# A linear attention in levels of quarters in place of halves, a table cast in pieces, and a sum taken two steps sooner

## The reference

```python
def gla_scan(q, k, v, log_a, s0):
    ...
    def step(S, inp):
        qc, kc, vc, ac = inp
        bcum = jnp.cumsum(ac, axis=1)
        diff = bcum[:, :, None] - bcum[:, None, :]
        decay = jnp.exp(jnp.where(causal[None, :, :, None, None], diff, -jnp.inf))
        att = jnp.einsum('bijhd,bjhd->bhij', qc[:, :, None] * decay, kc)
        o = (jnp.einsum('bhij,bjhe->bihe', att, vc)
             + jnp.einsum('bihd,bhde->bihe', qc * jnp.exp(bcum), S))
        blast = bcum[:, -1]
        S = (jnp.exp(blast)[..., None] * S
             + jnp.einsum('bjhd,bjhe->bhde', kc * jnp.exp(blast[:, None] - bcum), vc))
        return S, o
```

## Time and profile before

| | us |
|---|---|
| median of 3 runs | 1818.34 (1818.22 to 1819.02) |
| the profiled execution | 1818.22, of which 1816.4 are the span |
| PE busy | 1785.9 |
| DVE, ACT, POOL busy | 748.9, 509.3, 513.1 |
| a tile of the linear attention | 40.82, seven times from 907.22 to 1192.96; the first 40.62 |

### The profile page before, as it was taken

The page is one execution under the profiler, slowest core; times in us unless marked ns, Lnnn a source line. Parts: engine busy times, 40 slices in busy tenths (PEclk is TensorE's granted clock), DMA queues, the critical chain, the costliest instruction groups (busy, mean ns, idle before and its releaser), DMA issues.

```text
span 1816.4 us, 30442 instructions
## 1 busy us (share of the span) xinstructions
PE 1785.9 (98%) x11013; PEld 1663.2 (92%) x11013; DVE 748.9 (41%) x1517; ACT 509.3 (28%) x1205; POOL 513.1 (28%) x438
## 2 busy tenths in 40 slices
PE   6999999999999999999999999999999999999999
PEld 5999999989999999999999999999999888878887
DVE  7655540454434411111455554543221453453433
ACT  6311110134333410000344344430011343333332
POOL 4255430322232243342444444443324000000000
PEclk8999999999999999999999999999999999999999
DMA  7323211343444331221333432244443675664653
GB/s 258 134 79 86 80 51 38 97 110 101 111 112 118 92 110 54 80 71 53 110 85 93 116 98 84 84 126 148 143 123 113 209 253 163 206 221 163 197 168 133
DMA packets 245804, 221.10 MB, mean 122 GB/s; under 512 B 25857, under 2 KB 210337, under 8 KB 244274
## 3 DMA queue, kind: packets, MB, share of 16 engines
q1 hardware_dynamic: 171794, 177.07, 31.3%
q10 hardware_dynamic: 73944, 43.15, 8.7%
HBM read 170.03 MB, written 52.24 MB: 122 GB/s over the span
## 4 chain that ended last, share of the span: by engine, by line
PE 95%; DVE 2%; DMA 1%; ACT 1%; issue 0%; SPq 0%; POOL 0%; ACTq 0%; DVEq 0%
PE p L1717 20%; PE p L1719 19%; PE p L1718 19%; PE p L1808 7%; PE p L1810 7%; PE p L1812 7%; PE p L838 3%; PE p L581 1%; PE p L1752 1%; PE p L1751 1%; PE p L1753 1%; PE p L609 1%; PE p L593 1%; PE p L849 1%; PE p L856 1%; PE p L850 1%
## 5 line engine op out<-in xcount | busy, mean ns | idle before, releaser
L1717 PE MATMUL p<-x_hi,w_lo 128*128 128x384 f32 x2016 | 699.5, 347 | 0.0
L1719 PE MATMUL p<-x_hi,w_hi 128*128 128x384 f32 x2016 | 676.1, 335 | 0.0
L1718 PE MATMUL p<-x_lo,w_hi 128*128 128x384 f32 x2016 | 675.2, 335 | 0.0
L1717 PEld LDWEIGHTS p<-x_hi,w_lo 128*128 128x128 f32 x2016 | 379.8, 188 | 15.4 <-issue 13.3
L1718 PEld LDWEIGHTS p<-x_lo,w_hi 128*128 128x128 f32 x2016 | 380.0, 188 | 0.2
L1719 PEld LDWEIGHTS p<-x_hi,w_hi 128*128 128x128 f32 x2016 | 379.1, 188 | 0.0
L537 POOL TENSOR_TENSOR w_hi<-raw,small 128x512 fp32r<-128x512 f32 x164 | 174.2, 1062 | 724.5 <-PE p L1719 724.2
L541 POOL TENSOR_TENSOR w_lo<-raw,w_hi 128x512 fp32r<-128x512 f32 x164 | 215.1, 1312 | 12.9
L1997 DVE TENSOR_TENSOR w_lo<-raw,w_hi 128x512 fp32r<-128x512 f32 x192 | 132.2, 691 | 205.0 <-ACT w_hi L1665 205.0
L1665 ACT ACTIVATE w_hi<-raw 128x512 fp32r<-128x512 f32 x192 | 120.6, 631 | 240.5 <-PE p L1812 213.2
L1808 PE MATMUL p<-w_hi,x_lo 128*128 128x512 f32 x576 | 162.1, 390 | 1.1 <-DVE w_lo L1997 1.1
(11 more groups left out here) (174 smaller groups left out, 1753.7 us busy)
## 6 DMA issues: line engine op xcount, KB each, us to landing
raw<-in_w_out SPq DMA_DIRECT2D x192, 256.0 KB, 3.3
raw<-in_w_in SPq DMA_DIRECT2D x164, 256.0 KB, 4.5
h_t<-xn SPq DMA_DIRECT2D x126, 192.0 KB, 1.9
work<-h_t SPq DMA_DIRECT2D x24, 384.0 KB, 6.0
out<-work SPq DMA_DIRECT2D x36, 256.0 KB, 4.5
work<-h_t ACTq DMA_DIRECT2D x16, 512.0 KB, 5.3
work<-h_t ACTq DMA_DIRECT2D x32, 256.0 KB, 3.7
work<-in_x_prompt SPq DMA_DIRECT2D x32, 256.0 KB, 4.9
```

Of the source, the lines that this page charges most:

```text
L1717: pe.matmul(out, w_lo[:, k, :], x_hi[:, k, tok], start=(k == 0), stop=False)
L1718: pe.matmul(out, w_hi[:, k, :], x_lo[:, k, tok], start=False, stop=False)
L1719: mm = pe.matmul(out, w_hi[:, k, :], x_hi[:, k, tok], start=False, stop=(k == KT - 1))
```

## The change

Levels are blocks of 4s tokens in quarters, for s = 32, 8 and 2, in place of halves of 64 to 1. At each level the queries of the second, third and fourth quarter meet the keys of the quarters before them: 6 of 16 quarter pairs, 192 columns a head (`PAIRS`). What is left is the diagonal and the pair of tokens 2m and 2m + 1; the odd queries, scaled by their own gate (`l_odd`), are put behind the queries, and the diagonal's product takes 192 columns a head (`SAME`). So a tile has 4 such products of 192 columns in place of 1 of 128 and 7 of 64, decode 3 in place of 5. POOL makes four subtractions a level, ACT two exps, DVE four multiplications and six masked copies. Keys are turned at step 18, values at 22, levels at 29, 33 and 41. In decode keys are at 16, two levels at 28 and 33, values at 38. The diagonal now waits for `l_odd`, whose exp ACT takes after DVE's gates and ahead of the load of the gates' inputs, the scaling, the store and the load of the values. The first level's buffers (`far` and the place of the tile's stored output) wait for that store (`sl_st`). DVE clears `far` once.

The table (now 2560 columns) is cast in five pieces of 512. In the item `J_ATT` alone, the last sum of squares of the item before is taken at k = 4 in place of 6, and the first scores at step 5 in place of 4.

```diff
-LEVELS = (64, 32, 16, 8, 4, 2, 1)
-DEC_LEVELS = (8, 4, 2, 1)
+LEVELS = (32, 8, 2)
+DEC_LEVELS = LEVELS[1:]
+SAME = 3 * P // 2
+PAIRS = 6 * P // 4
+QUAD_AT = (0, 3 * P // 4, 5 * P // 4)
...
+M_PIECE = 512
+N_PIECES = (M_ALL + M_PIECE - 1) // M_PIECE
...
+        l_qo = four(work[:, 0:N_GLA * SAME])
+        l_q, l_odd = l_qo[:, :, 0:P], l_qo[:, :, P:SAME]
...
+        same_bank = (ub[0], ub[4])
...
             def values():
                 pe.wait_ge(sl_v, 16 * t + 16)
                 pe.wait_ge(sl_on, 4 * t + 1)
+                if dec:
+                    pe.wait_ge(sl_cp, len(LEVELS) * t + 1)
...
             def diagonal():
                 pe.wait_ge(sl_q, 16 * t + 16)
                 pe.wait_ge(sl_k, 16 * t + 16)
-                pe.wait_ge(sl_la, t + 1)
+                pe.wait_ge(sl_la, 2 * t + 2)
+                pe.wait_ge(sl_og, 4 * t + 1)
                 for h in range(N_GLA):
-                    hs = slice(h * P, h * P + P)
-                    mm = pe.matmul(ub[0][:, hs], l_k[:, hs], l_q[:, hs], start=True, stop=True)
+                    mm = pe.matmul(same_bank[h // 2][:, (h % 2) * SAME:(h % 2) * SAME + SAME], l_k[:, h * P:h * P + P],
+                                   l_qo[:, h, :], start=True, stop=True)
                 mm.then_inc(sl_dg, 1)
...
             def level(i):
                 s = levels[i]
                 pe.wait_ge(sl_zz, NZ * t + (i + 3))
-                if i == 1:
+                if s == LEVELS[1]:
+                    pe.wait_ge(sl_on, 4 * t + 1)
+                    if not dec:
+                        pe.wait_ge(sl_vtok, 2 * t + 2)
+                else:
                     pe.wait_ge(sl_ktok, t + 1)
-                if i >= 2:
-                    pe.wait_ge(sl_cp, len(LEVELS) * t + (i - 1))
+                    pe.wait_ge(sl_dcp, t + 1)
+                    if s == LEVELS[2] and not dec:
+                        pe.wait_ge(sl_cp, len(LEVELS) * t + 1)
+                at = quad_bank(s)
                 for h in range(N_GLA):
-                    z = l_z[(i + 1) % 2][:, h * P:h * P + P]
-                    mm = pe.matmul(ub[4 - i % 2][:, h * 64:h * 64 + 64], z, halves(z, s)[:, :, 1, :],
-                                   start=True, stop=True)
+                    mm = pe.matmul(ub[at + h // 2][:, (h % 2) * PAIRS:(h % 2) * PAIRS + PAIRS],
+                                   l_k4[s][:, h * P:h * P + P], l_q4[s][:, h, :], start=True, stop=True)
                 mm.then_inc(sl_p, 1)
...
-            stages = {6: logits, 14: diagonal, 22: keys, 30: values, 47: outputs}
+            stages = {6: logits, 14: diagonal, 18: keys, 22: values, 47: outputs}
             if not first:
                 stages[9] = linear_stages(pe, t - 1)[-1]
-            for i, step in enumerate((23, 25, 28, 32, 35, 38, 42)):
+            for i, step in enumerate((29, 33, 41)):
                 stages[step] = lambda i=i: level(i)
...
+                act.wait_ge(sl_la, 2 * t + 1)
+                act.activation(l_odd, odd(four(l_e[1])), ACT.Exp, scale=1.0 / TAU).then_inc(sl_a, 1)
...
+                act.wait_ge(sl_d, (NZ - 1) * t + (i + 2))
+                e = blocks(l_k4[s], s)[:, :, 0:3 * s]
+                act.activation(e, e, ACT.Exp, scale=-1.0 / TAU)
+                e = l_q4[s].rearrange("p h n -> p (h n)")
+                self.exp(t, i + 2, e, e, 1.0)
...
                     self.load_v(t)
                     self.decays(t)
+                    self.keys(t)
                     self.level(t, 0, LEVELS[0])
-                    self.keys(t)
-                    for i in range(1, 4):
-                        self.level(t, i, LEVELS[i])
+                    self.values(t)
 
                 def part_1():
-                    self.values(t)
-                    for i in range(4, 7):
+                    for i in range(1, len(LEVELS)):
                         self.level(t, i, LEVELS[i])
 
                 def part_2():
...
+                dve.memset(far, 0.0)
...
-                dve.copy_predicated(l_att, tables_sb[:, M_DIAG:M_DIAG + 512], ub[0][:, :]).then_inc(sl_dcp, 1)
+                for h in range(2):
+                    ins = dve.copy_predicated(two_heads(l_att, h), two(tables_sb[:, M_DIAG:M_DIAG + 2 * P]),
+                                              two(same_bank[h][:, 0:2 * SAME])[:, :, 0:P])
+                    ins.then_inc(sl_half, 1)
+                for h in range(2):
+                    dve.wait_ge(sl_half, HALVES * t + (h + 1))
+                    dve.nop(nofuse=True)
+                    ins = dve.copy_predicated(odd(two_heads(l_att, h)), two(tables_sb[:, 0:M_QUAD]),
+                                              two(same_bank[h][:, 0:2 * SAME])[:, :, P:SAME])
+                ins.then_inc(sl_dcp, 1)
...
-                self.copy_diagonal(t)
+                dve.wait_ge(sl_a, 4 * t + 4)
+                dve.wait_ge(sl_q, 16 * t + 16)
+                dve.tensor_tensor(l_odd, odd(l_q), l_odd, ALU.mult).then_inc(sl_la, 1)
...
+                self.copy_diagonal(t)
...
+                z, k = (blocks(x, s)[:, :, 0:3 * s] for x in (l_k4[s], l_k))
+                dve.tensor_tensor(z, k, z, ALU.mult)
+                for b in range(3):
+                    z = paired(l_q4[s], s, b)
+                    ins = dve.tensor_tensor(z, later(l_q, s, b), z, ALU.mult)
+                ins.then_inc(sl_zz, 1)
...
+                for at, b in enumerate((0, 2) if one_seq else (0, 1, 2)):
+                    n = s if one_seq else (3 - b) * s
+                    for h in range(2):
+                        if at:
+                            dve.wait_ge(sl_half, done + (2 * at + h - 1))
+                            dve.nop(nofuse=True)
+                        ins = dve.copy_predicated(
+                            later(two_heads(l_att, h), s, b)[:, :, :, 0:n], paired(mask, s, b)[:, :, :, 0:n],
+                            paired(two(ub[quad_bank(s) + h][:, 0:2 * PAIRS]), s, b)[:, :, :, 0:n])
+                        if b < 2:
+                            ins.then_inc(sl_half, 1)
+                ins.then_inc(sl_cp, 1)
...
                 def part_0():
                     self.gates(t)
                     self.level(t, 0, LEVELS[0])
-                    for i in range(1, 4):
+
+                def part_1():
+                    for i in range(1, len(LEVELS)):
                         self.level(t, i, LEVELS[i])
                         self.take(t, i - 1, LEVELS[i - 1])
-
-                def part_1():
-                    for i in range(4, 7):
-                        self.level(t, i, LEVELS[i])
-                        self.take(t, i - 1, LEVELS[i - 1])
+                    self.take(t, 2, LEVELS[2])
 
                 def part_2():
-                    self.take(t, 6, LEVELS[6])
                     self.state(t)
                     self.variance(t)
...
-            for i, (n, at) in enumerate([(n, n - 1)] + [(2 * s, s - 1) for s in levels]):
-                if i:
-                    pool.wait_ge(sl_zz, NZ * t + i)
-                b = l_b.rearrange("p (m n) -> p m n", n=n)
-                pool.tensor_tensor(l_e[(i + 1) % 2].rearrange("p (m n) -> p m n", n=n), b,
-                                   b[:, :, at:at + 1].to_broadcast([P, 4 * P // n, n]), ALU.subtract)\
-                    .then_inc(sl_d, 1)
+            pool.wait_ge(sl_a, 4 * t + 4)
+
+            b = l_b.rearrange("p (m n) -> p m n", n=n)
+            pool.tensor_tensor(l_e[1].rearrange("p (m n) -> p m n", n=n), b,
+                               b[:, :, n - 1:n].to_broadcast([P, 4 * P // n, n]), ALU.subtract).then_inc(sl_d, 1)
+            for s in levels:
+                if s == LEVELS[1]:
+                    pool.wait_ge(sl_zz, NZ * t + 2)
+                    pool.wait_ge(sl_kt, t + 1)
+                else:
+                    pool.wait_ge(sl_st, 16 * t + 16)
+                    if s == LEVELS[2] and n == P:
+                        pool.wait_ge(sl_p, len(LEVELS) * t + 1)
+                e, b = (x.rearrange("p (m q n) -> p m q n", q=4, n=s) for x in (l_k4[s], l_b))
+                pool.tensor_tensor(e[:, :, 0:3, :], b[:, :, 0:3, :],
+                                   b[:, :, 0:3, s - 1:s].to_broadcast([P, P // s, 3, s]), ALU.subtract)
+                for c in range(3):
+                    x = later(four(l_b), s, c)
+                    ref = l_b.rearrange("p (h m n) -> p h m n", h=N_GLA, n=4 * s)[:, :, :, (c + 1) * s - 1:(c + 1) * s]
+                    ins = pool.tensor_tensor(paired(l_q4[s], s, c), x,
+                                             ref.to_broadcast([P, N_GLA, P // (4 * s), (3 - c) * s]), ALU.subtract)
+                ins.then_inc(sl_d, 1)
...
-                stages = {3: logits, 6: linear_stages(self.pe, T - 1)[-1], 12: diagonal, 18: keys, 32: values}
-                for i, step in enumerate((20, 22, 25, 28)):
+                stages = {3: logits, 6: linear_stages(self.pe, T - 1)[-1], 12: diagonal, 16: keys, 38: values}
+                for i, step in enumerate((28, 33)):
```

(76 more changed lines are left out.)

60 lines of the change are left out of this document (27 added, 33 removed).

## The result

The changed kernel takes 1829.88 us (median of 4 runs, 1826.74 to 1830.15), against 1818.28 of the kernel before: 1.0063 times the time, 95% interval 1.0048 to 1.0077. Slower by 0.6% or 11.6 us, where 7 us less were forecast. The profiled execution took 1829.84, its span is 1828.1.

What follows compares the result with a forecast made beforehand. PE, busy 98% of the span, was taken to bound the kernel. Terms 1.8 - 0.1 - 0.7 + 5.1 + 1.1 gave 7.2 us less than the profiled 1818.22, so 1811.0, range 1801 to 1820.

Steps and rivals of the forecast that it cites:

- the sum 1.8 - 0.1 - 0.7 + 5.1 + 1.1: Gains in us: seven later tiles, first tile, decode, the cast in pieces, the sooner sum in `J_ATT`; together 7.2.
- Products: PE's stages in a linear-attention tile: 192 columns cost 1.31 each, so 1.96 us less a tile.
- The values' wait: Values' stage moved from step 30 to 22: load lands at 17.1 in the tile, PE waits 1.7 us a tile.
- the load shares with the weights: Rival, tiles: store and load start behind SP's first weights, landing 8.8 after issue, wait 3.2; 1821.5 to 1840; chance 0.10.
- The estimate of half the rate: Tiles, weights taking half the transfer rate: load lands at 17.5 to 18, PE waits 2.1 to 2.6; 1813.8 to 1817.3.
- The first tile: First linear-attention tile: 1.96 gained, less 0.48 for clearing and 1.57 for the diagonal's wait: -0.1 us.
- Decode: Linear attention's decode: from 0.57 us less to 2 more, the middle taken as -0.7.
- The cast and the sum: Table cast in five pieces gains 5.1 us; sooner sum of squares in `J_ATT` gains 1.1.
- pieces in one: Rival, cast: POOL's pieces leave DVE no gap, PE waits 2.8, only 0.7 of 5.1 stays; 1815.4; chance 0.14.
- Narrow blocks: Rival, levels: narrow blocks cost POOL four times 2.3, last level some 3 us late in eight tiles; 1837; chance 0.06.

Runs made afterwards that it cites:

- the last run: Changed kernel with SP's weights behind the values' load, last level at 42 except first tile, decode's prompt-state store behind the keys' copy: 1803.53 us, ratio 0.9919.

## Why the prediction was wrong

The forecast rested on the sum 1.8 - 0.1 - 0.7 + 5.1 + 1.1; measured, the same terms are -13.9, -1.2, -1.2, 4.9 and 0.9, and 1.1 more is lost elsewhere.

*Products: right.* 1.31 for a stage of 192 columns was forecast and measured. A tile without a wait takes 39.02, where 40.82 - 1.96 = 38.86 was expected; the gain is there, 1.8 a tile, as soon as nothing waits.

*The values' wait: the mechanism right, its size wrong, and this is the step that failed.* The forecast had a wait of 1.7 a tile; it is 2.7 on average. Two terms of it were too small. The delay on ACT is not 0.85 but 1.2: behind the new exp there is also the issue of the gates' inputs, 0.35, which used to be out of the way while ACT waited for PE; I had counted the exp and not the rest of the queue. And the landing is 8.0 in the median, not 7.3, because the delay puts the store 0.6 behind the first weights where it had been 0.6 ahead. The forecast took the landing time as a property of the line, a little above the median. It is a property of the order: 8.0 with the store behind the weights, 6.9 with the store ahead of them, 4.9 with the weights held back. The store was late by the same order: the first level's operands were there at 21.9 in the tile, where the forecast had about 20. Behind the values' wait that did not show; with the values at step 27 it cost 1.6 to 2.0 a tile.

*What was not in the sum.* The falls of the clock. In the trace of before the longest wait that kept it was 1.8, and one of 3.50 lost it; I put the forecast's 1.7 on the safe side. Measured, the wait grew past that, and the clock fell in four tiles. (The side was not safe either: the last run lost the clock behind 1.84.) The seven waits are 18.6, with 0.17 each for the drain 19.8; less the gain of 7 x 1.8 = 12.6 that is 7.2. What is left of 13.9 is 6.7, 1.7 a fall, near the 1.57 of the one that is shown. So of the 15.7 between 1.8 gained and 13.9 lost, 7.9 is the longer wait, 6.7 the clock and 1.1 the products' gain.

*The rival "the load shares with the weights" is what happened*, to which 0.10 was given. It put the landing at 8.8 and the wait at 3.2, a little too much, and the price at 1821.5 to 1840; 1829.9 lies in it. My argument against it, that the weights ran beside the load before too, overlooked that the store ran ahead of them. The estimate of half the rate, from the rule of the Trainium skill ("DMA: Bandwidth & Descriptors", Queues, rings and completion order) that each transfer engine takes packets from the queues in turn, had the load land at 17.5 to 18 in the tile; it landed at 17.7 to 18.4 in six of the seven, 7.5 to 8.2 after its issue. By these numbers the rule was the better guide here than the median of the line.

*The first tile:* 1.2 lost where 0.1 was forecast. The diagonal's wait was 2.9 in this execution; in the run with the weights behind it was 1.7, near the forecast's 1.57, and the tile 40.83. The rest stands beside a load's issue on ACT ahead of the gates that took 1.76 in this trace and 0.53 in that of before. It took 1.86 with the cast and the sum alone too, so it does not need this change of the linear attention; why it is long in some executions and short in others stays open. *Decode:* 1.2 lost, inside the bounds of 0.57 gained to 2 lost. ACT's scaling there begins 7.4 into the item in place of 5.1, 2.3 later where the forecast had up to 2, and the keys wait 0.9. The issue of the state's store, which the last run moves, stands ahead of the exps in both traces and takes 1.38 in both.

*The cast and the sum: right.* 4.9 and 0.9 for 5.1 and 1.1. DVE got in between the pieces, so "pieces in one" falls:

```profile
70.38 0.97 DVE L1974 TENSOR_TENSOR sq_parts<-xn,sq_parts 128x384 fp32r<-128x384 f32 x1
```

against 3.30, beside five pieces on POOL that took 3.17 together (0.63 each, for 0.46 forecast). PE waited 1.17 and kept its clock. *Narrow blocks:* a level's four subtractions take 2.6, 3.3 and 2.7 on POOL at s = 32, 8 and 2 in the tile shown, for 2.3 forecast, and the narrowest blocks are no dearer than the widest by more than 0.1. That the last level's 0.25 to 0.4, once the values' wait no longer covers it, comes from these tenths is likely but not shown.

## What to carry to other kernels

A stage that is moved sooner needs its operand's landing at the new place, and the landing time of a transfer is not a number of its line: look which transfers of other queues are issued around it, in what order, and what a delay of some tenths on the issuing engine does to that order. Count every instruction behind the one that is put in, issues of transfers too. Loads that nobody needs soon, as the weights here (issued 9 into a tile before the change, first split by POOL at 27.9), are better issued behind those that are waited for: one wait on SP's queue turned a loss of 0.6% into a gain of 0.5%, and with two small moves 0.8%.

## What the runs showed of the hardware

A store of 512 KB landed 3.5 us after its issue with only the values' load behind it, 4.1 when four weight loads of 256 KB began 0.6 behind it and 6.0 when they began 0.6 ahead (medians).

PE's clock fell behind waits of 3.69, 2.56, 2.74 and 2.04 us, and did not fall behind waits of 2.46, 2.58 and 2.54 in the same execution. With the values at step 27 one of 1.94 lost it and one of 2.00 kept it. The wait of 1.84 in `J_ATT` kept it in nine of the ten traces and lost it in that of the last run. In three of the runs it also fell in the first tile soon behind a wait of 0.9 ahead of the logits; in four others such a wait kept it. So the length of a wait alone did not decide it up to 2.6; every such wait has to be priced with a chance of a fall, here 1.6 to 1.7 us each in the tiles of the changed kernel.

DVE's four multiplications of a level took 2.4 us with POOL idle through most of them and 5.4 beside POOL's splits of weights; its sum of squares took 3.30 beside one cast of 3328 columns on POOL and 0.97 beside five of 512.
